# Halves of attention outputs made inside their own stage, and a rotation done by copies, in a fused transformer kernel

## What is computed

```python
# sliding window attention: 4 key heads, 16 query heads of 64
o = jnp.einsum('bnkgij,bnjkd->bnikgd', p / denom, vb)
o = o.reshape(b, L, ATT_WIDTH) * jax.nn.silu(gate.astype(f32))
return o.astype(h.dtype) @ w_out
...
# differential attention: 8 heads, two maps of width 64 each
q = apply_rope(q.reshape(B, T, DA_HEADS, 2, DA_HEAD_DIM), cos, sin) * (DA_HEAD_DIM ** -0.5)
k = apply_rope(k.reshape(B, T, DA_HEADS, 2, DA_HEAD_DIM), cos, sin)
...
a = p[:, :, 0] - lam * p[:, :, 1]
...
o = rms_norm(o, subln) * (1.0 - lambda_init)
return o.reshape(B, T, DA_HEADS * 2 * DA_HEAD_DIM) @ w_o
...
def apply_rope(x, cos, sin):
    x1, x2 = jnp.split(x.astype(jnp.float32), 2, axis=-1)
    return jnp.concatenate([x1 * c - x2 * s, x2 * c + x1 * s], axis=-1)
```

## Time and profile before

| | |
|---|---|
| median of 3 runs | 2344.64 us (2343.29 to 2345.02) |
| profiled execution | 2347.38 us |
| its span in the trace | 2344.6 us |
| mean granted TensorE clock | 0.946 |
| busy: TensorE, weight loads, VectorE | 92%, 81%, 62% |
| busy: ScalarE, GpSimd | 44%, 2% |
| read from HBM | 166.58 MB, 72 GB/s over the span |
| matmuls at L1795 (rotations) | 128, half of them in differential attention |

### The profile page before, as it was taken

How to read it: one execution, slowest core, us unless ns; L and a number is a source line. 1 busy time by engine, 2 the same in 40 slices (tenths; PEclk the granted TensorE clock), 3 DMA queues, 4 the chain that set the end, 5 groups by cost and what they waited for, 6 DMA issues and landing times. The chain is left out here.

```text
span 2344.6 us, 40889 instructions
## 1 busy us (share of the span) xinstructions
PE 2160.0 (92%) x15019; PEld 1904.4 (81%) x15019; DVE 1461.8 (62%) x3057; ACT 1020.6 (44%) x1887; POOL 47.8 (2%) x37
## 2 busy tenths in 40 slices
PE   5999996988887799998999999989899889999998
PEld 3777775766666688877999999977777679999997
DVE  6778876456555677765566663359566656666522
ACT  4555554334444455554444432324455444443322
POOL 1000000000000000000000000112100000000000
PEclk8999997989998899998999999979999889999998
DMA  5533321343111211112233333411111123333330
GB/s 123 141 106 100 94 72 48 96 90 67 33 37 45 61 48 49 49 36 63 82 90 91 91 104 97 89 32 40 48 37 45 36 64 91 89 89 92 107 97 36
DMA packets 353416, 170.30 MB, mean 73 GB/s; under 512 B 59711, under 2 KB 351400, under 8 KB 353320
## 3 DMA queue, kind: packets, MB, share of 16 engines
q1 hardware_dynamic: 352680, 168.19, 26.2%
q0 software_dynamic: 640, 0.87, 0.3%
HBM read 166.58 MB, written 2.16 MB: 72 GB/s over the span
## 5 line engine op out<-in xcount | busy, mean ns | idle before, releaser
L300 PE MATMUL ps<-h_parts,parts 128*128 128x264 f32 (+3 forms) x8576 | 1313.9, 312 | 38.1 <-DVE h_parts L667 16.4
L300 PEld LDWEIGHTS ps<-h_parts,parts 128*128 128x128 f32 x8576 | 1177.2, 191 | 133.6 <-issue 43.2
L259 ACT ACTIVATE parts<-ring 128x1024 fp32r<-128x1024 f32 (+1 forms) x282 | 306.9, 1093 | 708.1 <-PE ps L300 478.9
L275 DVE TENSOR_TENSOR parts<-ring,parts 128x1024 fp32r<-128x1024 f32 (+1 forms) x266 | 336.7, 1270 | 181.4 <-ACT parts L259 179.8
L300 PE MATMUL ps<-wide_parts,parts 128*128 128x264 f32 (+3 forms) x1152 | 349.0, 303 | 0.0
L300 PE MATMUL ps<-up_hidden,parts 128*128 128x264 f32 (+1 forms) x1408 | 253.8, 283 | 1.7 <-PEq L2424 1.7
L300 PEld LDWEIGHTS ps<-wide_parts,parts 128*128 128x128 f32 x1152 | 219.4, 190 | 8.8
L300 PEld LDWEIGHTS ps<-up_hidden,parts 128*128 128x128 f32 x1408 | 216.9, 188 | 2.1 <-issue 2.1
L2407 DVE TENSOR_TENSOR up_u<-ps,norm_rstd 128x264 f32<-128x264 f32 (+2 forms) x176 | 74.9, 426 | 160.6 <-PE ps L300 153.2
L2678 DVE TENSOR_TENSOR res<-ps,res 128x264 f32<-128x264 f32 (+2 forms) x64 | 27.2, 429 | 99.2 <-PE ps L300 92.8
L300 PE MATMUL ps<-gated_high,parts 128*128 128x512 f32 x256 | 81.8, 400 | 3.4 <-DVE wide_parts L1224 3.4
(11 more groups left out here) (308 smaller groups left out, 2408.4 us busy)
## 6 DMA issues: line engine op xcount, KB each, us to landing
ring<-in_ffn_w_up SPq DMA_DIRECT2D x88, 512.0 KB, 3.8
ring<-in_ssm_w_in SPq DMA_DIRECT2D x48, 512.0 KB, 4.1
ring<-in_ffn_w_down SPq DMA_DIRECT2D x32, 704.0 KB, 4.6
ring<-in_da_w_qkv SPq DMA_DIRECT2D x24, 512.0 KB, 3.8
ring<-in_dsa_w_in SPq DMA_DIRECT2D x24, 512.0 KB, 3.8
ring<-in_att_w_in SPq DMA_DIRECT2D x40, 256.0 KB, 3.7
ssm_prefix<-prefix_rows SPq DMA_DIRECT2D x32, 256.0 KB, 4.0
ring<-in_ssm_w_out SPq DMA_DIRECT2D x16, 512.0 KB, 4.1
```

The costliest lines, as they stand in the source:

```text
L259: self.nc.scalar.activation(self.part(st, u, 0), self.slot(x, st.kt), ACT.Copy).then_inc(self.w_high, 1)
L275: self.nc.vector.tensor_tensor(self.part(st, u, 1), self.slot(u % st.ring, st.kt), self.part(st, u, 0).bitcast(F32), ALU.subtract).then_in ...
L300: m = self.nc.tensor.matmul(out, w[:, n], b, start=start and f == j == 0, stop=stop and f == st.kt - 1 and j == 2)
```

## The change

Four stages and the last down product are edited.

- **Sliding attention**: on TensorE `pv` moves from in front of `linear` to behind it. From step 1 on, ScalarE splits two finished output tiles per step in slot 2, behind `silu(s, 0)`, and VectorE their low halves behind `softmax(s, 0)` and `softmax(s, 1)`. In the last step the output product's first two weights are split too. `project` gets `made=(heads, 6)` and splits only tiles 6 and 7, into a tensor of its own.
- **Differential attention**: `rot` goes. `turn(i, u)` on ScalarE issues four copies, SBUF to SBUF, each of 32 partitions by 528 numbers, that write `raw` with its blocks of 32 swapped to `turned`; the sine's table now carries the sign. The heads' splits stand in slot 3 of steps 3 to 8 on ScalarE and behind `softmax` of tile 1 on VectorE; the first two output weights in the last step.
- **Index stage**: the turns run in the order 0, 1, 4, 2, 3. The sparse projection's first two high halves are made in the value stage.
- **Last down product**: one range of 512 columns instead of two of 256.

```diff
@@ -70,7 +70,7 @@
         if d < 32:
-            rot2[b + d + 32, m] = -1
+            rot2[b + d + 32, m] = 1
         else:
@@ -81,6 +81,7 @@
     cos2, sin2 = np.cos(ang).astype(np.float32), np.sin(ang).astype(np.float32)
+    sin2 = np.where(d < 32, -1, 1).astype(np.float32)[:, None] * sin2
     return np.concatenate([eye, ones, tri, rot1, rot2, before, causal, cos2, sin2, inv1], axis=1)
@@ -278,7 +279,7 @@
     def high_first(self, act, st):
-        for u in range(st.depth):
+        for u in range(st.pre, st.depth):
             self.high(act, st, (0, u))
@@ -1518,11 +1517,11 @@
                             scores(s, q - 2)
+                        linear(chunk)
+                        if q == 0 and s:
+                            pv(s - 1, 2), trans(s - 1, 3)
                         if q >= 4:
                             pv(s, q - 4)
-                        linear(chunk)
-                        if q == 0 and s:
-                            trans(s - 1, 3)
                         if q == 1 and s:
@@ -1596,6 +1595,11 @@
                             silu(s, 0)
+                            for f in range(2 * s - 2, 2 * s) if s else ():
+                                act.wait_ge(sem["out"], f + 1)
+                                spread.act(act, f)
+                        if last and q in (3, 4):
+                            k.high(act, nxt, (0, q - 3))
                         if q == 3 and not last:
@@ -1685,10 +1689,14 @@
                             k.low_on_vector(dve, st, st.after(0, more[n - 4 + len(more)], st.depth))
+                        if n < 2 and s:
+                            spread.dve(dve, 2 * s - 2 + n)
+                        if last and n in (2, 3):
+                            k.low_on_vector(dve, nxt, (0, n - 2))
                     if last:
...
                         out(s)
-                for u in range(st.depth):
+                for u in range(st.pre, st.depth):
                     k.low_on_vector(dve, st, (0, u))
@@ -1932,7 +1942,10 @@
                     if u < 2:
-                        wait(act, sem["rot"], 2 * i - 1 + u if not isinstance(i, int) or i else 0)
+                        if diff:
+                            wait(act, s_turned[u], 64 * i)
+                        else:
+                            wait(act, sem["rot"], 2 * i - 1 + u if not isinstance(i, int) or i else 0)
                         wait(act, sem["cos"], 2 * i - 1 + u if not isinstance(i, int) or i else 0)
@@ -1940,6 +1953,13 @@
                     nc.scalar.activation(dst, ps[:, bank, 0:HALF], ACT.Copy).then_inc(sem["lin_free"], 1)
+
+                def turn(i, u):
+
+                    act.wait_ge(sem["lin_free"], NP * i + 2 * u + 2)
+                    wait(act, sem["rope"], 2 * i - 1 + u if not isinstance(i, int) or i else 0)
+                    for r in range(0, P, 32):
+                        act.dma_start(turned[r ^ 32:(r ^ 32) + 32, u, :], raw[r:r + 32, u, :]).then_inc(s_turned[u], 16)
 
@@ -1983,6 +2003,8 @@
                                 k.high(act, st, st.after(i, j // 2, st.depth))
+                                if diff and j < 4:
+                                    turn(i, j // 2)
 
@@ -2024,6 +2046,11 @@
                                 take_sum(s - 1)
+                            if q == 3 and tail and norm:
+                                act.wait_ge(sem["out"], s - 1)
+                                spread.act(act, s - 2)
+                            if q in (2, 3) and not lin:
+                                k.high(act, nxt, (0, q - 2))
                         if att:
@@ -2072,8 +2100,12 @@
                     for q in range(2):
-                        dve.wait_ge(sem["rot"], 2 * s + q + 1)
-                        do(v.tensor_tensor(both(t2), ps[:, 4 - 2 * q:6 - 2 * q, 0:HALF], both(sin), ALU.mult))
+                        if diff:
+                            dve.wait_ge(s_turned[q], 64 * s + 64)
+                            do(v.tensor_tensor(t2, turned[:, q, :], sin, ALU.mult))
+                        else:
+                            dve.wait_ge(sem["rot"], 2 * s + q + 1)
+                            do(v.tensor_tensor(both(t2), ps[:, 4 - 2 * q:6 - 2 * q, 0:HALF], both(sin), ALU.mult))
                         v.tensor_tensor(rop[:, q, :], t1[:, q, :], t2, ALU.add).then_inc(sem["rope"], 1)
@@ -2095,6 +2127,8 @@
                             k.low_on_vector(dve, st, st.after(s + 1, n - 3, st.depth))
+                            if isinstance(s, int) and s == NI - 1:
+                                k.low_on_vector(dve, nxt, (0, n - 3))
                         if not diff and n == 2:
@@ -2113,12 +2147,14 @@
                             head_norm(s - 2)
+                        if diff and norm and n == 1:
+                            spread.dve(dve, s - 2)
                     steps.end()
...
                     dve.wait_ge(sem["sheet"], 2)
-                for u in range(st.depth if diff else 0):
+                for u in range(st.pre, st.depth if diff else 0):
                     k.low_on_vector(dve, st, (0, u))
@@ -2165,6 +2201,8 @@
 
+    turns = [0, 1, 4, 2, 3]
+
     def sync_program(sp):
@@ -2183,13 +2221,14 @@
     def pe_program(pe):
-        def rotate(j):
-
+        def rotate(i):
+
+            j = turns[i]
             if j == 4:
...
                 pe.wait_ge(s_free, 2 * order.index(j) + 2)
-            wait(pe, s_rope, j)
+            wait(pe, s_rope, i)
             for b in range(2):
@@ -2302,8 +2341,7 @@
                     nc.scalar.activation(vT[:, j % 2, b * HALF:(b + 1) * HALF], ps[:, 4 + b, 0:HALF], ACT.Copy).then_inc(s_vfree, 1)
-                if j + 2 < 8:
-                    k.high(act, vst, divmod(j + 2, 4))
+                k.high(act, *((vst, divmod(j + 2, 4)) if j + 2 < 8 else (nxt, (0, j - 6))))
                 if j:
@@ -2327,7 +2365,9 @@
         do(v.tensor_tensor(rsin[:], k.sin2, k.rstd[:], ALU.mult))
-        for j, u in enumerate([0, 1, 2, 3, 4]):
+        for j, u in enumerate(turns):
+            if j == 4:
+                evict(wiT, 5)
             if u == 4:
@@ -2615,9 +2654,13 @@
         }
+        last = len(SWA_UNITS) - 3
+        S["swa_out"].slots, S["swa_out"].pre = [S["swa"].slots[x % 3] for x in (last, last + 1)], 2
+        S["da_out"].slots, S["da_out"].pre = S["da"].slots[0:2], 2
         for l in range(2):
...
             S[f"down{l}"].slots, S[f"down{l}"].pre = [6 * KT * P - 2 * FK * P, 0], 1
+        S["dsa"].slots = [2 * 2 * KT * P, 0]
         S["idx"].slots, S["idx"].pre = [2 * 2 * KT * P, 0, 2 * KT * P], 1
@@ -2690,14 +2733,21 @@
                     norm, Scaled(k, norm, S["ssm_out"], lambda f: gated[:, f, :], wide_low1))
-        swa(k, S["swa"], following["swa"], Residual(k, SEQ, y1, V_POST, r1, lambda j: k.wide[:, 20 + j, 0:SEQ],
-                                                    lambda f: k.wide[:, f, 0:SEQ], V_PRE + 8, r1, 5))
-        project(k, "swa_out", S["swa_out"], following["swa_out"], 1, wide1, (parts1[1], wide_low1), SEQ, to_y, y_tile)
-        pairs(k, "da", S["da"], following["da"], True, Residual(k, T2, y1, V_POST + 8, r1, lambda j: k.wide[:, 20 + j, 0:SEQ],
-                                                                lambda f: k.wide[:, f, :], V_DA, r2, 6))
+        with ExitStack() as own:
+            swa_high = k.sb("swa_high", [P, KT, SEQ], F32R, own)
+            update = Residual(k, SEQ, y1, V_POST, r1, lambda j: k.wide[:, 20 + j, 0:SEQ], lambda f: k.wide[:, f, 0:SEQ], V_PRE + 8, r1, 5)
+            heads = Spread(k, KT, wide1, lambda f: swa_high[:, f, :], wide_low1)
+            swa(k, S["swa"], following["swa"], update, heads)
+            project(k, "swa_out", S["swa_out"], following["swa_out"], 1, None, None, SEQ, to_y, y_tile, made=(heads, 6))
         with ExitStack() as own:
             da_high = k.sb("da_high", [P, KT, T2], F32R, own)
-            normed = project(k, "da_out", S["da_out"], following["da_out"], 1, wide2, (lambda f: da_high[:, f, :], wide_low2), T2, to_res, res_tile, gain=V_FFN)
+
+            def one_tile(x):
+                return lambda f: x[:, bass.ds(f, 1), :].rearrange("p a t -> p (a t)")
+            update = Residual(k, T2, y1, V_POST + 8, r1, lambda j: k.wide[:, 20 + j, 0:SEQ], lambda f: k.wide[:, f, :], V_DA, r2, 6)
+            heads = Spread(k, KT, one_tile(k.wide), one_tile(da_high), one_tile(k.wide_parts))
+            pairs(k, "da", S["da"], following["da"], True, update, spread=heads)
+            normed = project(k, "da_out", S["da_out"], following["da_out"], 1, None, None, T2, to_res, res_tile, gain=V_FFN, made=(heads, 6))
         if done("da"):
@@ -2721,7 +2771,7 @@
             return
-        ffn(1, normed, None, TAIL, [(META, SEQ // 2), (META + SEQ // 2, SEQ // 2)], META)
+        ffn(1, normed, None, TAIL, [(META, SEQ)], META)
         if done("ffn1"):
```

28 lines of the change are left out of this document (14 added, 14 removed).

## The result

| | before | changed |
|---|---|---|
| median of 4 runs | 2344.83 us | 2311.39 us (2311.34 to 2315.46) |
| ratio | | 0.9862, 95% interval 0.9845 to 0.9880 |
| span of the profiled execution | 2344.6 us | 2309.4 us |

A forecast was written before the change was run, and what follows sets the result against it. TensorE, busy 92% of the span, was taken as the bound, so its waits and own work decide. The terms summed to −35.2 us, from a median of 2344.64 to 2309.4 us, range 2297.5 to 2328.

The forecast's parts named there:

- Sliding attention: Products behind `pv`'s old place cover TensorE's waits and lift the slow clock: gross 21.9 us, splits cost 4.3, net −17.6.
- Starts of the output products: TensorE starts both output products earlier, with weights and six tiles or heads' halves ready: −4.1 us sliding, −4.4 us differential.
- Differential attention: Copies replace eight matmuls a head, gaining 1.6 us; issues and splits delay tile 2 in slot 3: −2 us in all.
- bound of +8: Upper bound of the differential attention term: issues of 0.6 us make a turn 2.4 us, about +8 in all.
- Rival A: ScalarE's issues cost next to nothing: differential term −9.5 us, sum −42.7, time 2302 us; chance 0.17.
- Index stage: The key's turn, third instead of last, covers its 4.04 us wait with two turns: −2.6 us, bounds 0 and −4.
- Sparse projection: Two high halves made in the value stage cut the 5.05 us wait, stores delayed 2.1: −2.4 us, bounds 0 and −5.
- Last down product: 528 matmuls of 512 columns replace 1056 of 256: 2.4 us saved, 0.3 lost at the last eviction, −2.1.
- B: ScalarE limits sliding attention (−9 us) and its issues cost 0.6 us (differential +8): 2328 us; chance together with D 0.24.
- C: Slower than before: a ScalarE issue costs 1.6 us, sum +24, 2368 us; decides from about 1.1 us; chance 0.04.
- D: Turned tile lands late or first output weights are missing; start gains of 8.5 us go, near −27; with B 0.24.

The follow-up runs named there:

- e7: Changed kernel with sliding attention's `pv` in front of the products again, splits kept: 2338.02 us, ratio 0.9958.
- e5: Changed kernel without the output halves inside both attention stages; the first two output weights still made ahead: 2305.18 us, ratio 0.9829.
- e11: Changed kernel with the turns issued by SyncE and no splits inside either attention stage: 2304.77 us, ratio 0.9823.
- e6: Changed kernel with turns issued by SyncE, ScalarE's differential split at the end of slot 2, VectorE's sliding splits one tile later: 2305.03 us, ratio 0.9815.
- e10: Changed kernel with turns issued by SyncE, the differential split at the end of slot 2, no splits in sliding attention: 2300.60 us, ratio 0.9803.
- e9: The changed kernel unaltered, run again beside three other variants: 2314.03 us, ratio 0.9867.
- e1: Changed kernel with the rotation of differential attention back on TensorE instead of the copies, all splits kept: 2310.53 us, ratio 0.9842.
- e3: Changed kernel with the turn's four copies issued by SyncE instead of ScalarE: 2303.29 us, ratio 0.9814.
- e2: Changed kernel with ScalarE's differential split moved from slot 3 to the end of slot 2: 2303.17 us, ratio 0.9810.
- e8: Changed kernel with index stage order, sparse projection's first weights and last down product as before the change: 2319.02 us, ratio 0.9882.
- e12: Changed kernel with one turn a head, q and k together, in slot 5, and ScalarE's differential split at the end of slot 2: 2301.25 us, ratio 0.9806.
- e4: Changed kernel with one turn a head of four copies, q and k together, issued in slot 5: 2303.43 us, ratio 0.9806.

## Why the prediction was right or wrong

**Sliding attention: mechanism right, size too small.** `pv` behind the products hid the waits and gave the slow clock back, as forecast. I put the gross gain at 21.9 us; e7 measures 24.5. And I charged the splits 4.3 us; e7 leaves 1.9. The two errors add up to the 5 us. How much of the 1.9 is the splits' own stays open: e5, without them, is 2.7 us shorter by its clock, and e11, with the same code, 2.0 us longer. By steps, 0 and 1 gained 17.1 us (forecast 14.8) and the last two 5.6 (forecast 2.8). In those I let only 2.8 us of the 6.13 be covered and took 2.1 back for a late mask; the wait for masks did come, 1.91 us, but the wait for `swa_pt` behind it went altogether, since what is late for one is then ready for the other. Two waits in a row on one chain are not two costs: with splits early, late or absent, the waits for masks and `swa_pt` together are 9.7, 11.4 and 11.0 us (changed, e6, e5).

**Starts of the output products: right**, −4.0 and −4.0 for −4.1 and −4.4. What I had not split is whose they are: e5 gives two thirds to the weights and 1.35 us to the six halves.

**Differential attention: the wrong sign, +5.8 for −2.** The place was right, slot 3 ahead of tile 2, and so was the chain. Three sizes in it were off. The issue was taken at 0.373 us, the commonest SP row, and measured 0.612; my bound held it, but I chose by frequency and not by likeness of the transfer. That was almost undone by the 0.9 us that the issues ran beside the weight's half: a turn held ScalarE 1.7 us, forecast 1.5. The gain from the matmuls was 30.98 − 29.61 = 1.4 us a head (e10), forecast 1.6. So a head with its split lost 0.6, forecast 0.2. Head 1, without one, gained 1.0 in this trace and 0.3 in e9's, forecast 1.4.

These sizes are the smaller part of the 7.8 us between forecast and trace. The step that failed is the sum over the heads: head 0 got the gain of any head without a split and the last head nothing, and this stage had no term for the clock. Head 0 was to gain 1.4 and lost 1.7. The windows account for it: 5 us at 0.50 and 5 at 0.88 are 3.1 us of full clock that before had, less the 1.4 won by the matmuls. In e10 the same ten us stand at 0.66 and 1.00, 1.7 us less 1.4, and head 0 is 0.3 longer than before (29.96). In e1, without any copy, the clock was 0.66 there too, and head 0 took 31.1. It took 31.1 in e3 as well, where SyncE issues the copies, and 30.2 in e5, where ScalarE does, so ScalarE's turn in front of the eviction is not what made head 0 long. Why the clock stood lower there stays open. The last head lost 1.0 (24.94 for 23.96), forecast nothing. And one head took 33.11 us, 1.5 more than its neighbours, at a clock of 0.66 for some of it; e9's trace has no such head, but 0.7 and 0.8 us more in two others, so that both stretches are 245.3.

One of the prediction's own figures is not consistent either. Its bound of +8 for issues of 0.6 us adds +1.1 for the two heads without a split; by its own chain they still gain 0.5 each, which makes the bound about +4.5.

**Why turn and split cost more together than apart.** Over a floor of 29.61 us a head, the turn alone costs 0.24 (e2, e5), the split in slot 3 alone 0.2 (e3), and both 2.0 (changed). The chain to tile 2 had 1.2 us of slack. The turn alone, 1.70 us, and the split alone, 0.63 + 0.70, each overrun it by 0.5 us or less; together, 3.0, they overrun it by 1.8. That is an estimate from these rows, and it agrees with the three periods. The forecast did use that slack once for the sum of both, but judged the whole as nearly free.

**The cost of an issue.** The Trainium skill, "DMA: Bandwidth & Descriptors", section "Issuing engines are not separate DMA queues", calls the sequencer's time usually small beside the DMA itself. The rows show 0.61 beside 2.6 us to landing, for ScalarE and SyncE alike, and four in a row are 2.46, as long as the DMA. The 50 ns of the same page's "Anatomy of one DMA — SWDGE (gpsimd) path" stand for another path; no row here is near them. Rival A, built on cheap issues, is excluded.

**Index stage: the right size, by another way in part**: 2.6 us in e8; a further 1.0 in the trace was the clock of the trace before. I expected the wait for the key to shrink. It went, but only 0.7 us of its 4.05 did, since the last turn then waits 3.33 for VectorE; 1.3 came from the wait behind it (2.51 to 1.25) and 0.5 from the transposes there, which took 1.08 us and now take 0.60. **Sparse projection: −2.9 for −2.4**, by e8: 3.6 at its start less 0.7 for the stores that come late. I kept 2.1 us for those; the mechanism was there, at a third of the size.

**Last down product: nearly right.** The products gave −2.0 for −2.4, since a 512 column matmul took 0.2315 us and not 0.2308, and the wait over the last eviction grew by 0.34 for 0.3, together −1.7 for −2.1. The Trainium skill, "TensorE: Matmul & The Clock Gate", section "Back-to-back issue gap", has 2.5 ns beside the columns for the gap of a single matmul at full clock; by an estimate from that, the change would give 1.3 us less the eviction's 0.3. The windows give 2 × 0.1176 − 0.2315 = 3.7 ns a pair, and e8 the 2.0 us.

Of the rivals, half of B occurred: ScalarE's issues did cost 0.6 us, and the differential term came to +5.8, between the forecast's −2 and B's +8. Its other half, ScalarE as the limit in sliding attention (−9), did not. C needed 1.1 us an issue; the longest of ScalarE's took 0.617 in the changed kernel, though single ones took 1.7 to 2.0 us in e12 and e4. D did not occur: the copies landed within 4.5 us, and both starts won their 4.0.

## What to carry to other kernels

A DMA issue is work of the engine that issues it: 0.6 us each for these copies, at 66 and at 132 KB alike, and everything queued behind it waits. Give it to the queue behind which nobody stands, or make one issue of two. Before adding two pieces of work to one slot, read the slack of the tile that follows and charge the sum against it. And when a stage's output is prepared early, price weights and activations apart: here the weights gave two thirds of it for nothing, the halves one third at a cost that depended on where they stood. And before a few us of one trace are put down to an edit, read the granted clock of both stretches: here it made head 0's loss and one head of 33.11 us.
